# Down projection of a hybrid decoder layer: GpSimd forms the sums of weights, the products of doubly summed weights stand last, the last trip has one seven-product block, and the start has fewer constant matmuls

## The chip, the cores and the metric

The kernel runs on one core of one Trainium2 chip. The time is device microseconds (us) of one execution. Engines are named as in the profile: PE is TensorE (matmuls; PEld its weight loads), DVE is VectorE, ACT is ScalarE, POOL is GpSimd, SP is the engine that issues the DMAs.

## The reference

One pre-norm decoder layer over 256 tokens, all in float32: three token mixers on one input projection, gates, an output projection with residual, then a squared-ReLU MLP with residual and a final RMS norm. The change lies in the last line but one, in its second product.

```python
h = rmsnorm(x, norm_ffn_g[l])
x = x + jnp.square(jax.nn.relu(h @ w_up[l])) @ w_down[l]     # 256x2048 @ 2048x8192, 256x8192 @ 8192x2048
return rmsnorm(x, final_g)
```

## The kernel before

**Weights.** All weights stream through a ring of four slots of 128x1024 float32 (512 KB, a "slab"). SP loads slab s into `w_raw[s % 4]` (line 412 or 415) once DVE has finished the low part of slab s - 4 (semaphore `lo_done`). ACT rounds the slab to the fast matmul type, `w_hi` (line 503; line 501 for half a slab), DVE takes the rest, `w_lo = w_raw - w_hi` (line 729; line 726 for half), and PE multiplies high by high, high by low and low by high: three matmuls for each product. ACT and DVE prepare slab k + 3 in the step in which PE multiplies slab k. ACT may overwrite a slot of `w_hi` when PE reports the slab used (`slab_used`).

**The MLP.** The 8192 hidden columns are done in 4 chunks of 2048. A chunk has 4 trips of `up` (8 slabs each) and 2 trips of `down` (16 slabs each), so there are 8 down trips in all. A down trip makes 1024 output columns in two column groups n = 0 and 1, and takes its 16 slabs (n, i) in the order of `PAIR` and `PAIR_ENDS`.

**Blocks of seven products.** At steps k = 6, 10 and 14 of a down trip (`quads`; in the last trip 6 and 10 only) the slabs k and k + 1 hold the same rows of both column groups. With the two row tiles of each and the two token tiles they make a 2 by 2 by 2 block product, which is done with seven products (P1 to P7) in place of eight, in Strassen's manner: 21 matmuls of 128x512 in place of 24. `products_quad` issues them. Four of the products need sums of weights, `w_sums`, called T1, T3, T2, T4: T1 and T3 are differences of loaded weights (one 128x1024 operation, `forms_first`), T2 is made from T1 and T4 from T2 (a 128x512 operation each, `forms_second`). ACT rounds them two at a time (`forms_hi`, lines 509 and 511), DVE takes the rest (`forms_lo`, line 756, semaphore `t_lo`, two counts for each block). P5 uses T1, P7 uses T3, P6 uses T2, P4 uses T4.

**Order of the work.** Everything is written by hand, engine by engine, and runs in program order on each engine. In the block that closes a trip (k = 14), P2, P4 and P3 come first, since they finish the four accumulators of the ordinary products (`c_full`), which DVE empties (`corner_sums`, line 790) before the next trip writes them; the other four products end in banks that `token_sums` (lines 772 to 783) empties after the block.

**The start.** Six constant matmuls stand before the first two groups of transposes of x and `WARM_GAP` = 20 of them (line 1400) between the second and the third group.

Of the kernel before, what the change touches and what calls it, by code (L numbers as in the profile page):

```python
# [141 lines left out]
def pair_of(c, t):  # L142

    return c * PH["down"].trips + t
# [15 lines left out]
WARM_GAP = 20  # L160
# [48 lines left out]
def build(nc, x, norm_mix_g, w_in, gate_b, conf_dw, conf_ln_g, conf_ln_b, w_conf_out, sconv_w,  # L209
# [5 lines left out]
    with ctx:  # L215
# [132 lines left out]
        def wide_rows(slab):  # L348

            return slab.rearrange("p (k b) n -> p k (b n)", k=DKT)  # L350
# [26 lines left out]
        def _(sp):  # L377
# [4 lines left out]
            def load_slab(ph, c, t, k):  # L382
# [102 lines left out]


        @block.scalar
        def _(act):
# [228 lines left out]
        def _(dve):  # L717
# [13 lines left out]
            def forms_first(ph, c, t, k):  # L731

                x, y = k % RING, (k + 1) % RING
                quad = quad_of(ph, c, t, k)
                if not (isinstance(quad, int) and quad == 0):
                    dve.wait_ge(t_lo, quad * 2)
                dve.wait_ge(raw_full[x], raw_count(ph, c, t, k))
                dve.wait_ge(raw_full[y], raw_count(ph, c, t, k + 1))
                left = w_raw[:, x:x + 2, 0:2, :].rearrange("p s k b -> p s (k b)")
                dve.tensor_tensor(w_sums[:, T1:T3 + 1, :], wide_rows(w_raw[:, y]), left, ALU.subtract).then_inc(t_raw, 1)  # L740

            def forms_second(ph, c, t, k):

                x, y = k % RING, (k + 1) % RING
                quad = quad_of(ph, c, t, k)
                dve.wait_ge(t_raw, quad * 2 + 1)
                dve.tensor_tensor(w_sums[:, T2, :], half_rows(w_raw[:, y], 1), w_sums[:, T1, :],
                                  ALU.subtract).then_inc(t_two, 1)
                dve.wait_ge(t_two, quad + 1)
                dve.tensor_tensor(w_sums[:, T4, :], half_rows(w_raw[:, x], 1), w_sums[:, T2, :],  # L750
                                  ALU.subtract).then_inc(t_raw, 1)

            def forms_lo(ph, c, t, k, part):
                dve.wait_ge(t_hi, quad_of(ph, c, t, k) * 2 + part + 1)
                two = slice(2, 4) if part == 0 else slice(0, 2)
                dve.tensor_tensor(w_forms[:, 1, two, :], w_sums[:, two, :], w_forms[:, 0, two, :].bitcast(F32),
                                  ALU.subtract).then_inc(t_lo, 1)
# [291 lines left out]
            def trip(ph, c, t):  # L1049
# [4 lines left out]
                for k in range(ph.nslabs):  # L1054
# [15 lines left out]
                    if k + 3 in quads(ph, c, t):  # L1070
                        forms_second(ph, c, t, k + 3)
# [3 lines left out]
                    if k + 4 in quads(ph, c, t):  # L1075
                        forms_first(ph, c, t, k + 4)
# [190 lines left out]
        def _(pe):  # L1267
# [58 lines left out]
            def products_quad(ph, c, t, k):  # L1326
# [22 lines left out]

                pe.wait_ge(lo_done, s + 1)  # L1350
                product(4, whole(0, 2 * i + 1), loaded(w_x, 1), False, closing)
                pe.wait_ge(t_lo, quad * 2 + 1)
                last = product(5, whole(1, 2 * i + 1), summed(T4), False, closing)
                if closing:
                    last.then_inc(c_full, 1)
                pe.wait_ge(lo_done, s + 2)
                pe.wait_ge(f_lo, c * 4 + i // 2 + 1)
                last = product(6, form(S4), loaded(w_y, 1), False, closing)
                if closing:
                    last.then_inc(c_full, 1)  # L1360
                if first and not (isinstance(c, int) and c == 0 and isinstance(t, int) and t == 0):
                    pe.wait_ge(p_sum, pair_of(c, t) * P_SUMS)
                product(P_BANK["P1"], whole(0, 2 * i), loaded(w_x, 0), first, final).then_inc(slab_used, 1)
                product(P_BANK["P6"], form(S2), summed(T2), first, final)
                pe.wait_ge(t_lo, quad * 2 + 2)
                product(P_BANK["P7"], form(S3), summed(T3), first, final)
                product(P_BANK["P5"], form(S1), summed(T1), first, final).then_inc(slab_used, 1)
# [208 lines left out]
```

## Time and profile before

| | |
|---|---|
| median of 3 runs | 1520.77 us (1520.45 to 1520.98) |
| the profiled execution's own time | 1521.96 us |
| its span, first to last instruction | 1519.9 us |
| PE busy | 1505.6 us |
| PEld busy | 1270.0 us |
| DVE busy | 1190.9 us |
| ACT busy | 756.1 us |
| POOL busy | 2.0 us |
| mean granted TensorE clock | 0.998 |

A row of the timeline gives the start and the duration in us from the span's start, the engine, the line of the kernel, what is written and read, and in brackets how long the engine had been idle and which event ended that. A PE row lasts longer than its share of the engine, since matmuls are pipelined: the distance between starts is what one costs.

### The profile page before, as it was taken

To read this page: it belongs to the slowest core of one execution; us is meant where nothing else is said; L and a number is where in the kernel's file an instruction comes from. 1 tells how busy PE (TensorE), PEld (TensorE's weight loads), DVE (VectorE), ACT (ScalarE), POOL (GpSimd) and SP (SyncE) were. 2 spreads that over 40 slices of the span, in tenths; PEclk is the share of its full clock that TensorE was granted. 3 is DMA by queue.
4 is the path that set the end of the run, shared out by engine and by line. 5 is a ranking of instruction groups with operands and counts; after the bars stand their busy time and mean duration, and the time that the engine had idled before them with its cause. 6 is when DMAs were issued, how large, how long until landed. Compare 5 with 4: busy or idle time off the path is not lost. (4 is left out here: it accounts for less than half of the span.)

```text
span 1519.9 us, 22403 instructions
## 1 busy us (share of the span) xinstructions
PE 1505.6 (99%) x7670; PEld 1270.0 (84%) x7670; DVE 1190.9 (78%) x1578; ACT 756.1 (50%) x942; POOL 2.0 (0%) x11
## 2 busy tenths in 40 slices
PE   9999999999999999999999999999999999999997
PEld 8888888877778888888888888888888888888885
DVE  6568888988889877565556779987798779887798
ACT  5544444465554455444445445545455545544553
POOL 0000000000000000000000000000000000000000
PEclk9999999999999999999999999999999999999999
DMA  7655566655556556656555655655656565566553
GB/s 240 194 180 190 187 195 199 196 182 173 171 171 193 194 194 211 194 195 199 181 180 171 197 186 208 207 190 170 207 190 211 170 211 199 181 196 203 204 198 138
DMA packets 209961, 290.86 MB, mean 191 GB/s; under 512 B 9227, under 2 KB 129107, under 8 KB 209778
## 3 DMA queue, kind: packets, MB, share of 16 engines
q1 hardware_dynamic: 209906, 290.14, 58.2%
q8 instruction: 33, 0.54, 0.2%
q14 instruction: 22, 0.18, 0.0%
HBM read 287.48 MB, written 2.10 MB: 191 GB/s over the span
## 5 line engine op out<-in xcount | busy, mean ns | idle before, releaser
L503 ACT ACTIVATE w_hi<-w_raw 128x1024 fp32r<-128x1024 f32 x510 | 532.8, 1056 | 458.0 <-PE acc L1321 266.2
L729 DVE TENSOR_TENSOR w_lo<-w_raw,w_hi 128x1024 fp32r<-128x1024 f32 x510 | 614.6, 1221 | 170.6 <-ACT w_hi L503 165.8
L1297 PE MATMUL acc<-h_hl,w_hi 128*128 128x512 f32 x1740 | 546.7, 395 | 0.0
L1295 PEld LDWEIGHTS acc<-h_hl,w_lo 128*128 128x128 f32 x1740 | 322.3, 188 | 72.7 <-issue 0.6
L1295 PE MATMUL acc<-h_hl,w_lo 128*128 128x256 f32 x1740 | 343.6, 279 | 0.0
L1297 PEld LDWEIGHTS acc<-h_hl,w_hi 128*128 128x128 f32 x1740 | 265.2, 189 | 0.0
L1319 PE MATMUL acc<-w_hi,m_hl 128*128 128x512 f32 x456 | 177.8, 390 | 0.0
L1321 PE MATMUL acc<-w_hi,m_hl 128*128 128x512 f32 x456 | 177.4, 389 | 0.0
L1320 PE MATMUL acc<-w_lo,m_hl 128*128 128x512 f32 x456 | 177.4, 389 | 0.0
L1319 PE MATMUL acc<-w_hi,h_hl 128*128 128x512 f32 x384 | 151.5, 394 | 0.0
L1321 PE MATMUL acc<-w_hi,h_hl 128*128 128x512 f32 x384 | 149.6, 389 | 0.0
L1320 PE MATMUL acc<-w_lo,h_hl 128*128 128x512 f32 x384 | 149.5, 389 | 0.0
L869 DVE SCALAR_TENSOR_TENSOR conv<-glu,par,conv (+1 forms) x240 | 108.8, 479 | 7.0 <-DVE conv L869 5.8
L1321 PEld LDWEIGHTS acc<-w_hi,m_hl 128*128 128x128 f32 x456 | 85.6, 188 | 17.8
L1320 PEld LDWEIGHTS acc<-w_lo,m_hl 128*128 128x128 f32 x456 | 85.6, 188 | 17.7
L1319 PEld LDWEIGHTS acc<-w_hi,m_hl 128*128 128x128 f32 x456 | 85.6, 188 | 17.6
L1319 PEld LDWEIGHTS acc<-w_hi,h_hl 128*128 128x128 f32 x384 | 72.1, 188 | 17.1 <-DVE w_lo L729 2.7
L661 ACT ACTIVATE second<-acc 128x512 f32<-128x512 f32 x58 | 34.7, 599 | 102.6 <-PE acc L1297 102.6
L1321 PEld LDWEIGHTS acc<-w_hi,h_hl 128*128 128x128 f32 x384 | 72.1, 188 | 15.2
L1320 PEld LDWEIGHTS acc<-w_lo,h_hl 128*128 128x128 f32 x384 | 72.1, 188 | 14.4
L1191 DVE TENSOR_TENSOR pair<-acc,second 128x512 f32<-128x512 f32 x54 | 37.3, 691 | 55.0 <-ACT second L661 54.9
L698 ACT ACTIVATE m_hl<-pair 128x512 f32 (+1 forms) x32 | 20.2, 632 | 74.1 <-DVE pair L1242 74.1
(202 smaller groups left out, 1472.8 us busy)
## 6 DMA issues: line engine op xcount, KB each, us to landing
w_raw<-in_w_in SPq DMA_DIRECT2D x200, 512.0 KB, 3.5
w_raw<-in_w_up SPq DMA_DIRECT2D x128, 512.0 KB, 4.3
w_raw<-in_w_down SPq DMA_DIRECT2D x128, 512.0 KB, 4.4
w_raw<-in_w_mix_out SPq DMA_DIRECT2D x32, 512.0 KB, 3.6
w_raw<-in_w_sconv_out SPq DMA_DIRECT2D x16, 512.0 KB, 4.2
w_raw<-in_w_attn_out SPq DMA_DIRECT2D x16, 512.0 KB, 3.9
w_raw<-in_w_conf_out SPq DMA_DIRECT2D x16, 512.0 KB, 4.2
bias_row<-in_gate_b SPq DMA_DIRECT2D x12, 256.0 KB, 3.9
```

Source lines behind the costliest of these rows:

```text
L503: act.activation(w_hi[:, q], w_raw[:, q], ACT.Copy).then_inc(hi_done, 1)
L661: act.activation(second[:, :, :], acc[:, b:b + 2, SEQ:], ACT.Copy).then_inc(half_copied, 1)
L698: act.activation(m_hl[:, bass.ds(j * 2, 2), 0, :], pair[n][:, :, :], ACT.Copy).then_inc(hid_hi, 1)
L729: dve.tensor_tensor(w_lo[:, q], w_raw[:, q], w_hi[:, q].bitcast(F32), ALU.subtract).then_inc(lo_done, 1)
L869: dve.scalar_tensor_tensor(dst, src, w, dst, ALU.mult, ALU.add).then_inc(step, 1)
L1191: dve.tensor_tensor(dst, halves[0], second[:, :, :], ALU.add).then_inc(half_sum, 1)
L1295: pe.matmul(*narrow[m], start=False, stop=False)
L1297: last = pe.matmul(*wide[m], start=False, stop=final)
L1319: pe.matmul(acc[:, b + m, :], h_h, hi[:, a, :], start=first, stop=False)
L1320: pe.matmul(acc[:, b + m, :], h_h, lo[:, a, :], start=False, stop=False)
L1321: last = pe.matmul(acc[:, b + m, :], h_l, hi[:, a, :], start=False, stop=final)
```

## The change

The two operations of `forms_first` and `forms_second` move from DVE to POOL, which runs them for every block in a stream of its own, as soon as both slabs have landed and `forms_lo` has consumed the sums before. DVE keeps a wait for them: before it takes the low part of slab k + 3 in step k = block - 2. The loads of slab block + 4 (and of the third slab of each up or down trip) wait for one more `lo_done`, since POOL may still read the slot. ACT and DVE now round T1 and T3 first, T2 and T4 second. `products_quad` has a new order: in the blocks at k = 6 and 10 it is P2, P1, P3, P7, P5, P6, P4; in the closing block P2, P4, P3, P1, P7, P5, P6. The last trip has one block (k = 10) and treats slabs 6 and 7 with ordinary products. `WARM_GAP` is 6.

```diff
-    return (6, 10) if last_trip(ph, c, t) else (6, 10, 14)
+    return (10,) if last_trip(ph, c, t) else (6, 10, 14)
...
-WARM_GAP = 20
+WARM_GAP = 6
...
+                late = k - RING in quads(ph, c, t) or ph.name in ("up", "down") and k == 2
                 if not (isinstance(s, int) and s < RING or shared and k == KDOWN):
-                    sp.wait_ge(lo_done, s + (shared and k == KDOWN - 1) - (RING - 1))
+                    sp.wait_ge(lo_done, s + (shared and k == KDOWN - 1) + late - (RING - 1))
...
@@ block.gpsimd
+            def forms_first(ph, c, t, k):
+                x, y = k % RING, (k + 1) % RING
+                quad = quad_of(ph, c, t, k)
+                if not (isinstance(quad, int) and quad == 0):
+                    pool.wait_ge(t_lo, quad * 2)
+                pool.wait_ge(raw_full[x], raw_count(ph, c, t, k))
+                pool.wait_ge(raw_full[y], raw_count(ph, c, t, k + 1))
+                left = w_raw[:, x:x + 2, 0:2, :].rearrange("p s k b -> p s (k b)")
+                pool.tensor_tensor(w_sums[:, T1:T3 + 1, :], wide_rows(w_raw[:, y]), left, ALU.subtract).then_inc(t_raw, 1)
+
+            def forms_second(ph, c, t, k):
...
+                pool.wait_ge(t_raw, quad * 2 + 1)
+                pool.tensor_tensor(w_sums[:, T2, :], half_rows(w_raw[:, y], 1), w_sums[:, T1, :],
+                                  ALU.subtract).then_inc(t_two, 1)
+                pool.wait_ge(t_two, quad + 1)
+                pool.tensor_tensor(w_sums[:, T4, :], half_rows(w_raw[:, x], 1), w_sums[:, T2, :],
+                                  ALU.subtract).then_inc(t_raw, 1)
...
@@ forms_hi, ACT
                 if k + 2 in quads(ph, c, t):
-                    act.wait_ge(t_raw, quad_of(ph, c, t, k + 2) * 2 + 2)
+                    act.wait_ge(t_raw, quad_of(ph, c, t, k + 2) * 2 + 1)
+                    act.activation(w_forms[:, 0, 0:2, :], w_sums[:, 0:2, :], ACT.Copy).then_inc(t_hi, 1)
+                if k + 1 in quads(ph, c, t):
+                    act.wait_ge(t_raw, quad_of(ph, c, t, k + 1) * 2 + 2)
                     act.activation(w_forms[:, 0, 2:4, :], w_sums[:, 2:4, :], ACT.Copy).then_inc(t_hi, 1)
-                if k + 1 in quads(ph, c, t):
-                    act.activation(w_forms[:, 0, 0:2, :], w_sums[:, 0:2, :], ACT.Copy).then_inc(t_hi, 1)
...
@@ trip, DVE
-                    if k + 3 in quads(ph, c, t):
-                        forms_second(ph, c, t, k + 3)
+                    if k + 2 in quads(ph, c, t):
+                        dve.wait_ge(t_raw, quad_of(ph, c, t, k + 2) * 2 + 2)
                     if ph.name == "down" and k == 15 and not last_trip(ph, c, t):
                         corner_sums(c, t)
                     lo(ph, c, t, k)
-                    if k + 4 in quads(ph, c, t):
-                        forms_first(ph, c, t, k + 4)
...
@@ products_quad, PE
+                pe.wait_ge(lo_done, s + 1)
+                corner("P2")
+                if closing:
+                    corner("P4").then_inc(c_full, 1)
+                    corner("P3").then_inc(c_full, 1)
+                    shared("P1").then_inc(slab_used, 1)
+                    shared("P7")
+                    shared("P5")
+                    shared("P6").then_inc(slab_used, 1)
+                else:
+                    shared("P1").then_inc(slab_used, 1)
+                    corner("P3")
+                    shared("P7")
+                    shared("P5")
+                    shared("P6")
+                    corner("P4").then_inc(slab_used, 1)
```

In the new `products_quad`, P4 and P6 wait for `t_lo` at the block's second count, P7 and P5 at its first. Before, P4 waited for the first count and P7 for the second.

DVE's order in the first down trip, before the change, from the preparation of slab 6 to the second `forms_lo` of the block at k = 6 and on to the sums of the next block:

```order
L740 TENSOR_TENSOR w_sums<-w_raw 128x1024 [waits raw_full3,raw_full2]
L747 TENSOR_TENSOR w_sums<-w_raw,w_sums 128x512 [waits t_raw]
L750 TENSOR_TENSOR w_sums<-w_raw,w_sums 128x512 [waits t_two]
L729 TENSOR_TENSOR w_lo<-w_raw,w_hi 128x1024 [waits hi_done]
L726 TENSOR_TENSOR w_lo<-w_raw,w_hi 128x512 [waits hi_done]
L756 TENSOR_TENSOR w_forms<-w_sums,w_forms 128x1024 [waits t_hi]
L729 TENSOR_TENSOR w_lo<-w_raw,w_hi 128x1024 [waits hi_done]
L756 TENSOR_TENSOR w_forms<-w_sums,w_forms 128x1024 [waits t_hi]
L729 TENSOR_TENSOR w_lo<-w_raw,w_hi 128x1024 [waits hi_done]
L740 TENSOR_TENSOR w_sums<-w_raw 128x1024 [waits raw_full3,raw_full2,t_lo]
```

The same stretch of DVE after the change (`t_raw` is POOL's report that the sums are there):

```order
L766 TENSOR_TENSOR w_lo<-w_raw,w_hi 128x512 [waits hi_done,t_raw]
L774 TENSOR_TENSOR w_forms<-w_sums,w_forms 128x1024 [waits t_hi]
L769 TENSOR_TENSOR w_lo<-w_raw,w_hi 128x1024 [waits hi_done]
L774 TENSOR_TENSOR w_forms<-w_sums,w_forms 128x1024 [waits t_hi]
L769 TENSOR_TENSOR w_lo<-w_raw,w_hi 128x1024 [waits hi_done] x2
L766 TENSOR_TENSOR w_lo<-w_raw,w_hi 128x512 [waits hi_done,t_raw]
```

The three operations on `w_sums` have left DVE; the half slab's low part, on which the load of slab block + 5 waits, now waits for POOL's last sum, and both `forms_lo` stand behind it.

PE's first seven matmuls of the closing block of the first down trip, before:

```order
L1346 MATMUL acc<-w_hi,m_hl 128x512 [waits lo_done,hid_lo]
L1347 MATMUL acc<-w_lo,m_hl 128x512
L1348 MATMUL acc<-w_hi,m_hl 128x512
L1346 MATMUL acc<-w_forms,m_hl 128x512 [waits t_lo]
L1347 MATMUL acc<-w_forms,m_hl 128x512
L1348 MATMUL acc<-w_forms,m_hl 128x512
L1346 MATMUL acc<-w_hi,a_forms 128x512 [waits f_lo,lo_done]
```

and after:

```order
L1362 MATMUL acc<-w_hi,m_hl 128x512 [waits lo_done,hid_lo]
L1363 MATMUL acc<-w_lo,m_hl 128x512
L1364 MATMUL acc<-w_hi,m_hl 128x512
L1362 MATMUL acc<-w_forms,m_hl 128x512 [waits t_lo]
L1363 MATMUL acc<-w_forms,m_hl 128x512
L1364 MATMUL acc<-w_forms,m_hl 128x512
L1362 MATMUL acc<-w_hi,a_forms 128x512 [waits f_lo,lo_done]
```

P4 (the rows with `w_forms,m_hl`) stays the second product of the closing block. What has changed is the count of `t_lo` for which it waits: the first `forms_lo` before, the second now.

## Rows read from the trace of the kernel before

**Rows 1.** The page's busy times (engine, us, share, instructions)

```profile
PE 1505.6 (99%) x7670; PEld 1270.0 (84%) x7670; DVE 1190.9 (78%) x1578; ACT 756.1 (50%) x942; POOL 2.0 (0%) x11
```

**Rows 2.** Waits of PE's weight loads: total us, times, longest

```profile
PEld acc L1346 <- DVE w_forms L756: 3.7, 4, 2.1
```

**Rows 3.** DVE's timeline in the first down trip

```profile
917.18 1.23 DVE L740 TENSOR_TENSOR w_sums<-w_raw 128x1024 f32<-128x1024 f32 x1 [1.81 <-DMA w_raw<-in_w_down]
...
919.16 0.69 DVE L750 TENSOR_TENSOR w_sums<-w_raw,w_sums 128x512 f32<-128x512 f32 x1
...
920.90 0.68 DVE L726 TENSOR_TENSOR w_lo<-w_raw,w_hi 128x512 fp32r<-128x512 f32 x1
921.51 1.22 DVE L756 TENSOR_TENSOR w_forms<-w_sums,w_forms 128x1024 fp32r<-128x1024 f32 x1
922.64 1.22 DVE L729 TENSOR_TENSOR w_lo<-w_raw,w_hi 128x1024 fp32r<-128x1024 f32 x1
...
926.53 1.22 DVE L740 TENSOR_TENSOR w_sums<-w_raw 128x1024 f32<-128x1024 f32 x1 [0.40 <-DMA w_raw<-in_w_down]
...
930.26 0.69 DVE L726 TENSOR_TENSOR w_lo<-w_raw,w_hi 128x512 fp32r<-128x512 f32 x1
...
936.04 1.23 DVE L740 TENSOR_TENSOR w_sums<-w_raw 128x1024 f32<-128x1024 f32 x1 [0.55 <-DMA w_raw<-in_w_down]
...
940.37 1.22 DVE L756 TENSOR_TENSOR w_forms<-w_sums,w_forms 128x1024 fp32r<-128x1024 f32 x1
...
942.64 1.22 DVE L756 TENSOR_TENSOR w_forms<-w_sums,w_forms 128x1024 fp32r<-128x1024 f32 x1
...
948.64 0.68 DVE L772 TENSOR_TENSOR y_tok<-p_part,y_tok 128x512 f32<-128x512 f32 x1
```

**Rows 4.** PE's timeline in the same trip, around its three blocks

```profile
922.35 0.39 PE L1346 MATMUL acc<-w_hi,m_hl 128*128 128x512 f32 x1
...
932.55 0.39 PE L1346 MATMUL acc<-w_hi,m_hl 128*128 128x512 f32 x1
...
942.75 0.39 PE L1346 MATMUL acc<-w_hi,m_hl 128*128 128x512 f32 x1
...
943.43 0.39 PE L1346 MATMUL acc<-w_forms,m_hl 128*128 128x512 f32 x1
...
947.51 0.39 PE L1319 MATMUL acc<-w_hi,m_hl 128*128 128x512 f32 x1
```

**Rows 5.** DMA issues of line 412: ns min/median/max

```profile
L412 SPq DMA_DIRECT2D w_raw<-in_w_down x128: 367/372/382, 891.9 to 1492.9; - x128
```

**Rows 6.** A later trip: DVE's sums for its closing block, and PE there

```profile
1324.46 1.23 DVE L740 TENSOR_TENSOR w_sums<-w_raw 128x1024 f32<-128x1024 f32 x1 [0.87 <-DMA w_raw<-in_w_down]
...
1329.99 0.39 PE L1346 MATMUL acc<-w_hi,m_hl 128*128 128x512 f32 x1
```

**Rows 7.** POOL's groups: xcount | busy us, mean ns

```profile
L477 POOL MEMSET mask<- 128x384 f32 x1 | 0.4, 418 | 0.0
...
L475 POOL TENSOR_SCALAR_AFFINE_SELECT ident<-ident 128x128 f32<-128x128 f32 x1 | 0.3, 292 | 0.1
...
L1566 POOL MEMSET const-float32-1.0<- 128x1 f32 x1 | 0.1, 98 | 0.0
```

**Rows 8.** PE's timeline, first block of the last trip

```profile
1487.44 0.50 PE L1346 MATMUL acc<-w_forms,a_forms 128*128 128x512 f32 x1 [1.65 <-DVE w_forms L756]
```

**Rows 9.** Timelines of PE and DVE at the start

```profile
7.04 4.66 PE L1400 MATMUL acc<-ident,ones 128*128 128x128 f32 x40
11.53 1.04 PE L1370 MATMUL acc<-ident,y_tok 128*128 128x128 f32 x8
12.32 0.70 PE L1290 MATMUL acc<-h_hl,w_hi 128*128 128x512 f32 x2
...
9.09 1.23 DVE L822 TENSOR_TENSOR w_lo<-w_raw,w_hi 128x1024 fp32r<-128x1024 f32 x1
```

**Rows 10.** Loads of x: from issue to landing, five DMAs, issued 1.2 to 4.9

```profile
DMA to landing us min/median/max: 2.7/6.3/9.7
```

**Rows 11.** Busy by stretch: us, PE, PEld, DVE, ACT, POOL, PEclk

```profile
1510.00:1512.00 2.00, 0.18 (x1) 0.00 (x0) 1.83 (x7) 1.09 (x4) 0.00 (x0) 1.00 0.01 4
```

More of the change, by code:

```diff
@@ L484, in _, with trip @@
                                fill=MASKED, base=-1, pattern=[[1, BLK]], channel_multiplier=-1).then_inc(consts, 1)
+            def forms_first(ph, c, t, k):
[8 more added lines that the diff above has]
+            def forms_second(ph, c, t, k):
+                x, y = k % RING, (k + 1) % RING
+                quad = quad_of(ph, c, t, k)
+                pool.wait_ge(t_raw, quad * 2 + 1)
[4 more added lines that the diff above has]
+                                  ALU.subtract).then_inc(t_raw, 1)
+            def trip(ph, c, t):
+                if ph == "v tokens":
+                    return
+                for k in quads(ph, c, t):
+                    forms_first(ph, c, t, k)
+                    forms_second(ph, c, t, k)
+            trip(PH["down"], 0, 0)
+            with pool.Fori(1, PH["down"].trips) as t:
+                trip(PH["down"], 0, t)
+            with pool.Fori(1, CHUNKS - 1) as c:
+                with pool.Fori(0, PH["down"].trips) as t:
+                    trip(PH["down"], c, t)
+            for t in range(PH["down"].trips):
+                trip(PH["down"], CHUNKS - 1, t)
         @block.scalar
@@ L729, in lo @@
                     dve.tensor_tensor(w_lo[:, q], w_raw[:, q], w_hi[:, q].bitcast(F32), ALU.subtract).then_inc(lo_done, 1)
[L731 to L751, printed above, removed]
             def forms_lo(ph, c, t, k, part):
                 dve.wait_ge(t_hi, quad_of(ph, c, t, k) * 2 + part + 1)
-                two = slice(2, 4) if part == 0 else slice(0, 2)
+                two = slice(0, 2) if part == 0 else slice(2, 4)
                 dve.tensor_tensor(w_forms[:, 1, two, :], w_sums[:, two, :], w_forms[:, 0, two, :].bitcast(F32),
@@ L1348, in product, with corner @@
                     return pe.matmul(acc[:, at, :], rows[1], columns[0], start=False, stop=stop)
+                def corner(name):
+                    if name == "P2":
+                        return product(4, whole(0, 2 * i + 1), loaded(w_x, 1), False, closing)
+                    if name == "P3":
+                        pe.wait_ge(lo_done, s + 2)
+                        pe.wait_ge(f_lo, c * 4 + i // 2 + 1)
+                        return product(6, form(S4), loaded(w_y, 1), False, closing)
+                    pe.wait_ge(t_lo, quad * 2 + 2)
+                    return product(5, whole(1, 2 * i + 1), summed(T4), False, closing)
@@ new lines, in shared @@
+                def shared(name):
+                    if name == "P1":
+                        if first and not (isinstance(c, int) and c == 0 and isinstance(t, int) and t == 0):
+                            pe.wait_ge(p_sum, pair_of(c, t) * P_SUMS)
+                        return product(P_BANK[name], whole(0, 2 * i), loaded(w_x, 0), first, final)
+                    rows, f = {"P6": (S2, T2), "P7": (S3, T3), "P5": (S1, T1)}[name]
+                    pe.wait_ge(t_lo, quad * 2 + (2 if name == "P6" else 1))
+                    return product(P_BANK[name], form(rows), summed(f), first, final)
@@ L1350, in products_quad @@
                 pe.wait_ge(lo_done, s + 1)
-                product(4, whole(0, 2 * i + 1), loaded(w_x, 1), False, closing)
-                pe.wait_ge(t_lo, quad * 2 + 1)
-                last = product(5, whole(1, 2 * i + 1), summed(T4), False, closing)
+                corner("P2")
                 if closing:
[L1355 to L1366, printed above, removed]
```

1 line of the change is left out of this document (removed).

## The prediction

> **What bounds the kernel now.** I read the page first: PE is busy 1505.6 us of a span of 1519.9 [rows 1], and the rest lies at the two ends, so PE is the bound and the time changes where PE issues fewer matmuls or waits. The view of waits comes second. In all 23 blocks together PE's weight loads wait 3.7 us for `w_forms` [rows 2]; the largest stall of the matmuls, 1.65 us, is in the first block of the last trip [rows 8]. So there is little to win; what decides is whether the new order keeps PE fed.
>
> The DVE timeline of the first down trip beside PE's [rows 3, 4] shows how near the edge this is. The blocks start at 922.35, 932.55 and 942.75: 10.20 us apart, for 21 and 24 matmuls, so a matmul costs 10.20 / 45 = 0.227 us and a product of three 0.68. DVE's sums for them start at 917.18, 926.53 and 936.04, each time just as the second slab of the block lands (the DMA ends the idle time). These landings hang in a loop: slab 11 is loaded when the low part of slab 7 is done (920.90 + 0.68 = 921.58) and lands at 926.53, 4.95 later; slab 15 hangs on slab 11 in the same way (930.95 to 936.04, 5.09). The loop takes 9.35 to 9.5 us a turn, PE 10.20 a block: it has 0.7 to 0.85 us in hand per turn. At the closing block P4 starts at 943.43 and the `forms_lo` it needs ended at 940.37 + 1.22 = 941.59, 1.84 us earlier.
>
> **The sums on POOL.** The trace has no two-input operation of POOL, so the cost X of the three operations is bounded from both sides. As fast as DVE: 1.23 + 0.69 + 0.69, which the rows put from 917.18 to 919.85, 2.7 us. POOL's own rows [rows 7] are 98 ns for a memset of one element a partition, 418 for 384 (0.84 ns an element written) and 292 for an affine_select of 128, one input and one output: (292 - 98) / 128 = 1.52 ns an element. By that rate the 1024, 512 and 512 elements take 3 x 0.1 + 2048 x 0.00152 = 3.4 us. A second input is one more stream; at the price of the memset's stream, 0.84, the rate is 2.36 and X = 0.3 + 4.8 = 5.1 us. I take 5.1, since the operations do have two inputs and the nearest row has one; both ends stay for the range.
>
> The Trainium skill's page "GPSIMD Engine Reference", section 3.1, gives 4497 ns for a two-input operation of 2048 float32. Scaled to these sizes, an estimate from that page is X = 4.7, and the sum below would come to about 1547 in place of 1555.
>
> **What becomes of the loop.** In step block - 2 DVE now waits for POOL's last sum, then does the half slab, `forms_lo`, a slab, `forms_lo`. By the distances in [rows 3] (0.61, 1.13, 1.14 and 1.22 for the last) the half slab ends 0.68 and the second `forms_lo` 4.10 us after the sums. Both loads of the next block now wait for that half slab, so slab 11 is issued behind slab 10: 0.37 us more [rows 5], 5.3 us to landing. In the times of the first trip, with X = 5.1:
>
> - Block at 6: slab 7 lands 917.18 as before (it hangs on slab 3, untouched). Sums 922.28, half slab 922.96, second `forms_lo` 926.38. P6 is the sixth product and would start at 922.35 + 3.40 = 925.75: PE is 0.63 late.
> - Block at 10: landing 928.26, sums 933.36, half slab 934.04, second `forms_lo` 937.46, against 932.55 + 3.40 = 935.95: 1.5 late in all.
> - Closing block: landing 939.34, sums 944.44, second `forms_lo` 948.54. P4 is second here and needs it; it would start at 943.43: 5.1 us late in all.
>
> The turn is 5.3 + 5.1 + 0.7 = 11.1 us, slower than PE's 10.20, and P4 waits for the later of the two `forms_lo` where it waited for the earlier. The last block's end moves with 3X. In other trips the third landing is later against PE: 1329.99 - 1324.46 = 5.5 us ahead of the closing block [rows 6] against 6.7 in the first. Between them I add 0.4: 5.5 us a trip, 38.5 us in the 7 trips with three blocks. Three of these trips follow another down trip; there the late `token_sums` has been the brake on slab 3. They start 948.64 - 947.51 = 1.1 us after PE's end now; DVE has then also more time to be ready, about 0.5 us after PE's end, so 3 x 0.6 = 1.8 us comes back. Down trips cost +36.7 us.
>
> What DVE saves (2.7 us a block) buys nothing: it stands at the wait for POOL in that time. ACT's two roundings of sums keep their places; the first is ready before DVE needs it, the second before the second `forms_lo`, since a slab's low part stands between. The extra wait of the third slab's load in up and down trips is hidden: ACT wants that slab three steps of 2.72 us later, and a landing takes some 5.
>
> **The last trip.** Three more matmuls, +0.68; the wait of its first block goes, 1.65 idle plus 0.11 on the slower matmul, -1.8. Its one block at k = 10 is not behind a loop (slab 7 needs no sums), so POOL has time: slab 11 lands 5.3 us after the low part of slab 7, some 8 us ahead of the block. Together -1.1 us.
>
> **The start.** 40 rows of constant matmuls take 4.66 us, 28 of them 3.3 [rows 9]. The third part of x is issued at 2.7 and lands 6.3 later, at 9.0 [rows 10]; the transposes, now at 11.53, can start there and need 0.8. The first product then waits for the first low part, 9.09 + 1.23 = 10.32, and starts at about 10.4 in place of 12.32: -1.9 us, which the later slabs keep, since ACT and DVE move up with the transposes. It costs more than it gains only if the idle moments (8.4 to 9.0, 9.9 to 10.4) drop the clock. At the end of the program PE's last matmul ended at 1510.2 and the granted clock was still 1.0 up to 1512 [rows 11], so pauses of 0.6 us are short beside what it bore there.
>
> **Sum.** 36.7 - 1.1 - 1.9 = +33.7 on the profiled 1521.96, 1555.7; the median of the runs lies 1.2 below the profiled execution, so 1554.5, rounded to 1555.
>
> **Rivals.**
> - *POOL and DVE hold each other up.* Just before the second slab of a block lands, the first has landed and DVE takes its low part (1.22 us); if the two cannot run together, POOL starts some 1.0 us late in the second and third block, 2 us a trip, 14 us in all: 1569 with X = 5.1. For it: the two meet in every trip. Against it: no row of before has both busy. The Trainium skill's page "SBUF — State Buffer", "Who interferes with whom", says that a DVE instruction with two SBUF inputs and a GpSimd instruction that reads SBUF exclude each other, the later one waiting in full; that is this mechanism, and no row of before can show it. With the page's X as well the estimate would be about 1561.
> - *POOL is quick enough* (the other side). From X = 3.4 down the first trip's P4 is on time: 948.54 - 3 x 1.7 = 943.44 against 943.43. Then what is left is a second `forms_lo` that follows the low part of slab 16; in before it ended at 942.64 + 1.22 = 943.86 [rows 3], 0.4 after P4's start, and it can hardly be earlier than 943.5. So 7 x 0.1 to 0.4 is lost, 3.0 won at the ends and up to 0.9 from the waits of before: 1517.5 to 1520.5. For it: no row shows a slow POOL. Against it: already its one-input rate gives 3.4.
> - *The waits fall elsewhere*, so that the same X costs half: if slabs 10 and 11 land faster than 5 us, the loop has 0.5 us more a turn, 1 us a trip: 1548. It is in the range of the forecast.
>
> **Numbers.** POOL at 4.2 to 5.5 without mutual blocking, 1537 to 1563: 0.52. With blocking, 1556 to 1574: 0.33. POOL quick: 0.13, half of it within 0.2% (3 us, about what a measurement can tell from no change), half faster. Something else: 0.02. The range 1537 to 1572 leaves out the quick POOL and a little at the top. Faster 0.08, same 0.07, slower 0.85.
>
> **What would show it.** POOL's three operations take near 5 us for a block, not 2.7. PE waits for `w_forms` at the fourth matmul of the closing block in seven trips, 3 to 6 us of delay summed over each trip, and DVE's half slab waits for POOL. Slab 11 lands about 5.3 us after the half slab of 7. In the last trip no wait; the first product starts near 10.4 at full clock. If DVE rows of 128x1024 last over 1.3 us, or POOL's first sum starts later than its slab lands, the two block each other. I am wrong if X is below 3.5, or if POOL's sums start much earlier than the landings that DVE waits for now.

## The result, and the profile after

The changed kernel takes 1592.44 us (median of 4 runs, 1589.84 to 1594.64) against 1520.88 (1520.45 to 1522.96) before, on the same chip: a ratio of 1.0461, 95% interval 1.0449 to 1.0474. It is slower, as forecast, but by 71.6 us where 34 were forecast, and outside the range. The profiled executions differ by 68.1 us of span (1588.0 against 1519.9).

The page gives the busy times [rows 1 before] and the 40 slices of the span. A slice is 39.7 us, and the down trips lie from about 912 us on.

```profile
PE 1527.1 (96%) x7645; PEld 1273.9 (80%) x7645; DVE 1134.5 (71%) x1507; ACT 754.6 (48%) x940; POOL 120.2 (8%) x77
...
PE   9999999999999999999999989899889998899987
...
POOL 0000000000000000000000043001230012400121
```

PE's slices are below 9 only in the down part, eight of them, and in seven of the eight POOL has work. PE is "busy" for 21 us more with 25 matmuls fewer: some of them ran slower. The view of waits (engine, line, what is waited for: total us, times, longest) answers [rows 2]:

```profile
DVE w_lo L766 <- POOL w_sums L506: 115.8, 22, 6.0
...
PEld acc L1362 <- DVE w_forms L774: 55.4, 32, 5.3
...
PE acc L1362 <- DVE w_forms L774: 41.3, 23, 4.9
...
PE acc L1362 <- DVE w_lo L766: 5.7, 9, 1.3
```

DVE's half slab stands 22 times for POOL's last sum, and PE's weight loads stand 55.4 us for `w_forms`, 3.7 before. The 5.7 us for `w_lo` L766 is P3, waiting for the half slab, a wait that the prediction did not have. POOL's timeline in the first down trip shows the loop:

```profile
915.48 2.44 POOL L496 TENSOR_TENSOR w_sums<-w_raw 128x1024 f32<-128x1024 f32 x1 [912.71 <-DMA w_raw<-in_w_down]
917.99 1.30 POOL L503 TENSOR_TENSOR w_sums<-w_raw,w_sums 128x512 f32<-128x512 f32 x1
919.37 1.30 POOL L506 TENSOR_TENSOR w_sums<-w_raw,w_sums 128x512 f32<-128x512 f32 x1
926.97 3.18 POOL L496 TENSOR_TENSOR w_sums<-w_raw 128x1024 f32<-128x1024 f32 x1 [6.30 <-DMA w_raw<-in_w_down]
...
939.35 3.15 POOL L496 TENSOR_TENSOR w_sums<-w_raw 128x1024 f32<-128x1024 f32 x1 [6.42 <-DMA w_raw<-in_w_down]
```

and DVE's beside it, which answers to [rows 3]:

```profile
920.71 0.69 DVE L766 TENSOR_TENSOR w_lo<-w_raw,w_hi 128x512 fp32r<-128x512 f32 x1 [5.68 <-POOL w_sums L506]
...
926.63 1.22 DVE L769 TENSOR_TENSOR w_lo<-w_raw,w_hi 128x1024 fp32r<-128x1024 f32 x1 [0.69 <-ACT w_hi L542]
...
932.96 0.69 DVE L766 TENSOR_TENSOR w_lo<-w_raw,w_hi 128x512 fp32r<-128x512 f32 x1 [5.10 <-POOL w_sums L506]
...
938.98 1.22 DVE L769 TENSOR_TENSOR w_lo<-w_raw,w_hi 128x1024 fp32r<-128x1024 f32 x1 [0.79 <-ACT w_hi L542]
...
945.29 0.69 DVE L766 TENSOR_TENSOR w_lo<-w_raw,w_hi 128x512 fp32r<-128x512 f32 x1 [5.08 <-POOL w_sums L506]
...
948.17 1.22 DVE L774 TENSOR_TENSOR w_forms<-w_sums,w_forms 128x1024 fp32r<-128x1024 f32 x1
```

The three sums take 919.37 + 1.30 - 915.48 = 5.19 us. The half slab ends at 920.71 + 0.69 = 921.40, and the next sums start when the slab lands, 926.97: 5.57 later (5.70 in the next turn, 933.65 to 939.35). The turns are 11.49 and 12.38 us, against PE's 10.20. In the second and third block POOL's first sum starts while DVE is in the 1.22 us low part that began 0.34 and 0.37 us earlier, and lasts 3.18 and 3.15 in place of 2.44. Over the 14 turns of the seven trips with three blocks the turn is 12.29 us in the mean (11.49 to 13.08; 9.68 before), and the leg from the half slab's end to the landing is 6.12 (5.57 to 6.99; before, with the load issued alone, 5.27). The first trip is one of the milder ones. PE's timeline beside it, which answers to [rows 4]:

```profile
924.86 0.51 PE L1362 MATMUL acc<-w_forms,a_forms 128*128 128x512 f32 x1 [0.62 <-DVE w_forms L774]
...
933.70 0.50 PE L1362 MATMUL acc<-w_hi,a_forms 128*128 128x512 f32 x1 [0.38 <-DVE w_lo L766]
...
934.84 0.50 PE L1362 MATMUL acc<-w_forms,a_forms 128*128 128x512 f32 x1 [0.17 <-DVE w_forms L774]
...
937.11 0.50 PE L1362 MATMUL acc<-w_forms,a_forms 128*128 128x512 f32 x1 [0.61 <-DVE w_forms L774]
...
944.49 0.39 PE L1364 MATMUL acc<-w_hi,m_hl 128*128 128x512 f32 x1
949.44 0.79 PE L1362 MATMUL acc<-w_forms,m_hl 128*128 128x512 f32 x1 [4.56 <-DVE w_forms L774]
950.03 0.63 PE L1363 MATMUL acc<-w_forms,m_hl 128*128 128x512 f32 x1
950.46 0.63 PE L1364 MATMUL acc<-w_forms,m_hl 128*128 128x512 f32 x1
```

P6 is late in block 6, P3, P7 and P6 in block 10, and P4 in the closing block starts 949.44 - 944.49 - 0.23 = 4.72 us late; the five delays (start to start, less 0.227 for a matmul) add to 7.2 us. Behind P4 the matmuls stand 0.43 us apart in place of 0.227. The windows show why (the stretch, its length, busy of PE, PEld, DVE, ACT, POOL, then the granted clock; 1.00 is 2.4 GHz, 0.50 is 1.2 GHz; the last two are the share and GB/s of the DMAs):

```profile
941.00:944.00 3.00, 3.00 (x15) 2.49 (x14) 0.00 (x0) 1.47 (x2) 2.84 (x3) 1.00 0.13 51
944.00:949.00 5.00, 0.88 (x4) 0.38 (x3) 3.71 (x4) 2.54 (x3) 1.25 (x1) 1.00 0.33 97
949.00:952.40 3.40, 2.96 (x7) 2.38 (x8) 2.75 (x3) 0.00 (x0) 0.00 (x0) 0.50 0.95 357
952.40:956.00 3.60, 3.60 (x17) 2.96 (x17) 2.89 (x3) 2.26 (x3) 0.00 (x0) 1.00 0.29 111
```

PE was idle for 4.56 us, and the clock was at its lower level from 949.0 to 952.4. That happens at P4's wait in each of the seven trips with a closing block, beginning between 2.9 us before P4's start and 0.7 behind it, for 3.4 us in four of them and 6.8 us in three. By the distances between the starts of PE's matmuls in the down part, delays of over 0.06 us add to 60.4 us (3.1 before), and the slower matmuls to 11.0 us (0 before). This count takes in the matmul behind each late one, which is late too, by 0.11 us, or by 0.36 at the lower clock; with these the first trip has 8.0 us, not 7.2.

At the start the prediction's step held: twelve constant matmuls end early, the transposes start at 9.47 (9.0 was given), and the first product at 10.49 (12.32 in [rows 9]).

```profile
7.02 1.50 PE L1433 MATMUL acc<-ident,ones 128*128 128x128 f32 x12
9.47 1.09 PE L1403 MATMUL acc<-ident,y_tok 128*128 128x128 f32 x8 [0.95 <-DMA y_tok<-in_x]
10.49 0.70 PE L1306 MATMUL acc<-h_hl,w_hi 128*128 128x512 f32 x2
```

### The profile page after: what moved, and what is told of

Its sections match the earlier page's. It is cut to its first block and busy times, and to the rows that moved or that the text cites. A ratio compares the mean times of both kernels' runs of the same rounds, so it can differ in the third digit from the quotient of the medians.

```text
span 1588.0 us, 22392 instructions
## 1 busy us (share of the span) xinstructions
PE 1527.1 (96%) x7645; PEld 1273.9 (80%) x7645; DVE 1134.5 (71%) x1507; ACT 754.6 (48%) x940; POOL 120.2 (8%) x77
## 5 line engine op out<-in xcount | busy, mean ns | idle before, releaser
L1335 PE MATMUL acc<-w_hi,m_hl 128*128 128x512 f32 x464 | 180.9, 390 | 0.0
L1336 PE MATMUL acc<-w_lo,m_hl 128*128 128x512 f32 x464 | 180.6, 389 | 0.0
L1337 PE MATMUL acc<-w_hi,m_hl 128*128 128x512 f32 x464 | 180.6, 389 | 0.0
L496 POOL TENSOR_TENSOR w_sums<-w_raw 128x1024 f32<-128x1024 f32 x22 | 60.0, 2727 | 1436.2 <-DMA w_raw<-in_w_down 1436.2
L766 DVE TENSOR_TENSOR w_lo<-w_raw,w_hi 128x512 fp32r<-128x512 f32 x22 | 15.2, 693 | 115.8 <-POOL w_sums L506 115.8
(202 smaller groups left out, 1519.9 us busy)
```

Of the source, the lines that this page charges most:

```text
L496: pool.tensor_tensor(w_sums[:, T1:T3 + 1, :], wide_rows(w_raw[:, y]), left, ALU.subtract).then_inc(t_raw, 1)
L766: dve.tensor_tensor(half_rows(w_lo[:, q], 1), half_rows(w_raw[:, q], 1), half_rows(w_hi[:, q], 1).bitcast(F32), ALU.subtract).then_inc(lo_ ...
L1335: pe.matmul(acc[:, b + m, :], h_h, hi[:, a, :], start=first, stop=False)
L1336: pe.matmul(acc[:, b + m, :], h_h, lo[:, a, :], start=False, stop=False)
L1337: last = pe.matmul(acc[:, b + m, :], h_l, hi[:, a, :], start=False, stop=final)
```

## The experiments

Each time is a median, with its ratio to the kernel before, run beside it on the same chip (1522.99 to 1523.39 us). The changed kernel was run beside a before of 1520.88, so differences between it and the others are taken from the ratios (0.1% is 1.5 us). "Stalls" are the delays between matmul starts in the down part, counted as for the 60.4 us above, and "clock" is what the slower matmuls add, 11.0 there; both are of the one profiled execution.

### Which part of the change costs

**e1_ends_only**: the kernel before with the two changes at the ends.

```diff
-    return (6, 10) if last_trip(ph, c, t) else (6, 10, 14)
+    return (10,) if last_trip(ph, c, t) else (6, 10, 14)
-WARM_GAP = 20
+WARM_GAP = 6
```

> The kernel before with two parts of the change alone: 6 constant matmuls in place of 20 at the start, and one block in place of two in the last trip. My step: -1.9 us at the start and -1.1 us in the last trip, so about 1517.9 us (-0.2%). Rival: the pauses of PE at the start drop the clock, and the start gains nothing or loses up to 3 us, 1520 to 1523.

1519.76 us, 0.9976 (0.9967 to 0.9986): a gain of some 3.7 us; the prediction had 3.0.

**e2_sums_on_dve**: the changed kernel with `forms_first` and `forms_second` back on DVE, in their old places.

```diff
-                    if k + 2 in quads(ph, c, t):
-                        dve.wait_ge(t_raw, quad_of(ph, c, t, k + 2) * 2 + 2)
+                    if k + 3 in quads(ph, c, t):
+                        forms_second(ph, c, t, k + 3)
...
+                    if k + 4 in quads(ph, c, t):
+                        forms_first(ph, c, t, k + 4)
```

> The changed kernel with the three operations on sums of weights back on DVE in their old places; order of roundings, order of products, later loads and both ends as in the changed kernel. If POOL's slowness is the cause: only P4 of the closing block waits, for a second forms_lo that ended 0.4 to 1.7 us after P4's start in the trace of before, 0.9 a trip, 6.4 us in all, less 3 at the ends: 1522 to 1526 us. Rival, the new orders and the later loads are the cause: 1570 us or more.

1541.46 us, 1.0121 (1.0106 to 1.0137). So POOL is the larger part of the loss, 1.0461 against 1.0121 or 52 us, but 18 us are lost without it, which neither theory had. DVE's timeline of the same trip:

```profile
915.36 1.23 DVE L742 TENSOR_TENSOR w_sums<-w_raw 128x1024 f32<-128x1024 f32 x1 [1.74 <-DMA w_raw<-in_w_down]
...
925.36 1.23 DVE L742 TENSOR_TENSOR w_sums<-w_raw 128x1024 f32<-128x1024 f32 x1 [1.05 <-DMA w_raw<-in_w_down]
...
935.48 1.23 DVE L742 TENSOR_TENSOR w_sums<-w_raw 128x1024 f32<-128x1024 f32 x1 [1.17 <-DMA w_raw<-in_w_down]
...
942.08 1.22 DVE L758 TENSOR_TENSOR w_forms<-w_sums,w_forms 128x1024 fp32r<-128x1024 f32 x1
```

The turns are 10.00 and 10.12 us, where [rows 3] has 9.35 and 9.51. And P4 waits for the `forms_lo` that ends at 943.30:

```profile
941.17 0.39 PE L1350 MATMUL acc<-w_hi,m_hl 128*128 128x512 f32 x1
943.36 0.50 PE L1348 MATMUL acc<-w_forms,m_hl 128*128 128x512 f32 x1 [1.80 <-DVE w_forms L758]
...
944.96 0.63 PE L1348 MATMUL acc<-w_hi,m_hl 128*128 128x512 f32 x1
945.38 0.63 PE L1349 MATMUL acc<-w_lo,m_hl 128*128 128x512 f32 x1
```

A wait of 1.80 us was enough to be followed by matmuls 0.42 us apart. In this kernel the clock fell in four of the seven trips, behind delays of P4 of 1.95 to 2.7 us (start to start); behind the other three, 1.7 to 2.5 us, it did not. Stalls 18.2, clock 5.6.

**e9_later_loads_only**: the kernel before with the later loads. **e10_new_orders_on_dve**: e2 without them.

```diff
+                late = k - RING in quads(ph, c, t) or ph.name in ("up", "down") and k == 2
-                    sp.wait_ge(lo_done, s + (shared and k == KDOWN - 1) - (RING - 1))
+                    sp.wait_ge(lo_done, s + (shared and k == KDOWN - 1) + late - (RING - 1))
```

> The kernel before with the later loads alone (slab block + 4, and the third slab of each up or down trip, wait for one more lo_done). In e2 each turn of the loop from load to load was 0.65 us longer than before, 1.3 us by the closing block. In the kernel before P4 has 0.6 to 1.8 us in hand there, so this alone costs 0 to 2 us in all: 0 to +0.1%. Rival, the later loads cost by themselves what e2 lost: +8 us or more.

> e2 without the later loads: sums on DVE, new orders of roundings and products, both ends. P4 of the closing block waits for the second forms_lo, 0.4 to 1.7 us late, 6.4 us in all, and the ends give 3.6: +2 to +4 us against before (+0.1 to +0.3%), with the clock at 1.0 as no stall reaches 2 us. e2 lies at +1.2%; the difference of some 15 us is then what the later loads cost once P4 has no slack. Rival, the new order alone costs it: e10 at +1% or more.

e9: 1533.93 us, 1.0071 (1.0057 to 1.0085), where next to nothing was expected. e10: 1525.85 us, 1.0021 (1.0012 to 1.0030), as expected. With e2 they close the account of its 18 us. Against e1 the new orders cost 0.45%, 7 us, most of it P4's wait for the second `forms_lo` (stalls 6.6 against 1.8), and on top of that the later loads cost 1.0%, 15 us. In e9 they alone cost 11. The clock is enough to explain the difference: it costs 5.6 us in e2 and nothing in e9. Its turns, again by DVE's timeline:

```profile
917.41 1.23 DVE L741 TENSOR_TENSOR w_sums<-w_raw 128x1024 f32<-128x1024 f32 x1 [1.78 <-DMA w_raw<-in_w_down]
...
927.37 1.23 DVE L741 TENSOR_TENSOR w_sums<-w_raw 128x1024 f32<-128x1024 f32 x1 [1.00 <-DMA w_raw<-in_w_down]
...
937.28 1.23 DVE L741 TENSOR_TENSOR w_sums<-w_raw 128x1024 f32<-128x1024 f32 x1 [0.95 <-DMA w_raw<-in_w_down]
```

They are 9.96 and 9.91 us, 0.4 to 0.6 longer than before. Over the seven trips the landing leg is 5.92 us in the mean, 5.27 before, and eight of the 14 turns take longer than PE's 10.20 (11.09 at most).

**e13_late_in_down_only** and **e14_late_third_slab_only** split the later loads:

```diff
+                late = k - RING in quads(ph, c, t)               # e13
+                late = ph.name in ("up", "down") and k == 2      # e14
```

> Half of e9 on the kernel before: only the loads of slab block + 4 wait for one more lo_done. If e9's loss (+0.7%) comes from the longer turn of the load loop, it is all here: +0.5 to +0.8%. Rival, it comes from the third slab of each trip, which is loaded when DVE is busy with the end of the trip before: 0 to +0.2% here.

> The other half: only the third slab of each up and down trip waits for one more lo_done. By the longer turn of the load loop: 0 to +0.2%. By the rival (the third slab): +0.5 to +0.8%.

e13: 1532.83 us, 1.0062 (1.0049 to 1.0076), stalls 10.8. e14: 1524.25 us, 1.0005 (0.9996 to 1.0014). All of the loss is in the loads of slab block + 4; the wait of the third slab is hidden, as predicted.

### How much of it is POOL's duration

**e3_three_quarters** and **e4_half**: the changed kernel, in which POOL forms the sums for 384 or 256 of the 512 columns of each. The other columns of the sums are left out (they hold zeros).

```diff
-                pool.tensor_tensor(w_sums[:, T1:T3 + 1, :], wide_rows(w_raw[:, y]), left, ALU.subtract).then_inc(t_raw, 1)
+                pool.tensor_tensor(w_sums[:, T1:T3 + 1, 0:256], wide_rows(w_raw[:, y])[:, :, 0:256], left[:, :, 0:256], ALU.subtract).then_inc(t_raw, 1)
```

> The changed kernel with POOL working on 384 of each 512 columns (the sums of the other columns are left out and stand at zero). Everything else as changed. By the lengths of POOL's operations in the changed kernel (2.44 and 1.30 us, so 2.2 ns an element and 0.16 a call) the three take 4.1 us in place of 5.2. With the loop as the cause each trip is 3 x 1.1 = 3.4 us less late, about 4 us, no single stall is near 4.5 us and the clock stays at 1.0: 7 x 4 - 5 = +24 us, 1540 to 1550. Rival, a fixed cost of handing the sums between engines: 1570 us or more.

> The same with 256 of each 512 columns: POOL's three operations take 2.9 us, about what DVE needed. The loop then turns faster than PE, and the time falls to 1518 to 1524 us, near the kernel before. Rival, a fixed cost of handing over: the step from 384 to 256 columns brings as little as that from 512 to 384 did not, over 1550 us.

e3: 1570.83 us, 1.0319 (1.0303 to 1.0334). e4: 1537.25 us, 1.0090 (1.0074 to 1.0105). Both are well above what was expected, since the expectations had neither the cost of the later loads nor the clock. The time follows POOL's duration: three operations take 5.2 us, 4.1 (e3) and 2.95 (e4) where DVE is not beside them, and the ratios are 1.0461, 1.0319 and 1.0090. The steps are 22 and 35 us for a quarter each. POOL's timeline of e4:

```profile
917.94 1.31 POOL L496 TENSOR_TENSOR w_sums<-w_raw 128x512 f32<-128x512 f32 x1 [915.17 <-DMA w_raw<-in_w_down]
919.33 0.75 POOL L503 TENSOR_TENSOR w_sums<-w_raw,w_sums 128x256 f32<-128x256 f32 x1
...
927.35 2.05 POOL L496 TENSOR_TENSOR w_sums<-w_raw 128x512 f32<-128x512 f32 x1 [6.45 <-DMA w_raw<-in_w_down]
```

The second of the two large sums is again 0.7 us longer, though it has half the elements: what is added comes from DVE's operation and is no share of POOL's.

### POOL and DVE beside each other

**e12_no_dve_beside_pool**: the changed kernel, in which DVE takes the low part of slabs 10 and 14, the ones before the sums of the second and third block, for a single element of each partition; the rest of these low parts is left out.

```diff
+                elif k + LOOKAHEAD in (10, 14) and k + LOOKAHEAD in quads(ph, c, t):
+                    dve.tensor_tensor(w_lo[:, q, 0, 0:1], w_raw[:, q, 0, 0:1], w_hi[:, q, 0, 0:1].bitcast(F32),
+                                      ALU.subtract).then_inc(lo_done, 1)
```

> The changed kernel in which DVE's operation that meets POOL's first one (the low part of slabs 10 and 14 of a down trip) is cut to one element a partition; that part of the low weights is left out. If the two block each other and that has a price, POOL's first operation takes 2.45 us in all blocks and the half slab comes 0.7 us earlier in each turn, 1.4 us a trip, 10 us in 7 trips, some more if the clock falls for shorter: 1574 to 1584 us. Rival, the blocking hides behind other waits: 1590 us or more.

1583.11 us, 1.0389 (1.0373 to 1.0405), 0.7% or 11 us below the changed kernel, with an uncertainty of some 3 us. POOL's group of line 496 (xcount | busy us, mean ns), in e12:

```profile
L496 POOL TENSOR_TENSOR w_sums<-w_raw 128x1024 f32<-128x1024 f32 x22 | 54.4, 2472 | 1435.2 <-DMA w_raw<-in_w_down 1435.2
```

and in the changed kernel:

```profile
L496 POOL TENSOR_TENSOR w_sums<-w_raw 128x1024 f32<-128x1024 f32 x22 | 60.0, 2727 | 1436.2 <-DMA w_raw<-in_w_down 1436.2
```

POOL's operations are 5.6 us shorter in all, the profiled executions differ by 6.2 us of span (1588.0 and 1581.8), and the medians by 11. The rest need not be blocking: the mean clock was 0.983 to 0.987 in the runs of the changed kernel, with the profiled run at the upper end, and 0.987 to 0.989 in those of e12. The turns of the first trip are 11.6 and 11.7 without the second party (11.49 and 12.38 with it).

In the last trip of the changed kernel the two hold each other up in turn, first POOL behind DVE, then DVE behind POOL, then POOL again:

```profile
1553.86 3.08 POOL L496 TENSOR_TENSOR w_sums<-w_raw 128x1024 f32<-128x1024 f32 x1 [28.57 <-DMA w_raw<-in_w_down]
1555.61 2.41 DVE L769 TENSOR_TENSOR w_lo<-w_raw,w_hi 128x1024 fp32r<-128x1024 f32 x1 [0.97 <-ACT w_hi L542]
1557.02 2.17 POOL L503 TENSOR_TENSOR w_sums<-w_raw,w_sums 128x512 f32<-128x512 f32 x1
```

Without a meeting these take 2.44, 1.22 and 1.30 us. It is the sign that the prediction named, a DVE row of over 1.3 us.

**e6_dve_waits_earlier**: DVE waits for the sums one step earlier, so it has nothing to do while POOL works.

```diff
-                    if k + 2 in quads(ph, c, t):
-                        dve.wait_ge(t_raw, quad_of(ph, c, t, k + 2) * 2 + 2)
+                    if k + 3 in quads(ph, c, t):
+                        dve.wait_ge(t_raw, quad_of(ph, c, t, k + 3) * 2 + 2)
```

> The changed kernel; DVE waits for POOL's sums one slab earlier, so that no DVE operation runs beside POOL's first operation in the second and third block. If the two block each other on SBUF, POOL's operation of 128x1024 takes 2.45 us in all blocks, where it took 3.15 in the second and third; DVE's slab now stands behind it (1.14 us more to the half slab), so the time is a little worse than 1592, up to 1600. Rival, POOL's longer operation comes from the DMA landing beside it or from the data: it stays at 3.1 us in the second and third block.

1608.60 us, 1.0556 (1.0538 to 1.0573). POOL's first sum is at its short duration throughout, as expected:

```profile
929.34 2.44 POOL L496 TENSOR_TENSOR w_sums<-w_raw 128x1024 f32<-128x1024 f32 x1 [7.63 <-DMA w_raw<-in_w_down]
...
943.51 2.45 POOL L496 TENSOR_TENSOR w_sums<-w_raw 128x1024 f32<-128x1024 f32 x1 [8.95 <-DMA w_raw<-in_w_down]
```

But the turns are 12.84 and 14.17 (12.8 to 14.2 in all trips): the low part that had run beside POOL now runs behind it, and more loads hang on it. So it is no remedy, and the time was missed.

### The orders and the clock

**e5_old_order_pool**: the changed kernel with the old order of ACT's and DVE's roundings of the sums and of PE's products (P4 waits for the first `forms_lo` again; POOL's part and the loads stay).

```diff
-                corner("P2")
+                product(4, whole(0, 2 * i + 1), loaded(w_x, 1), False, closing)
+                pe.wait_ge(t_lo, quad * 2 + 1)
+                last = product(5, whole(1, 2 * i + 1), summed(T4), False, closing)
```

> The changed kernel with the old order of roundings (T2 and T4 first) and the old order of products in every block; POOL still makes the sums, ends and later loads as changed. P4 of the closing block then waits for the first forms_lo, which ends about 2.3 us after the sums, not 4.1. With the loop as the cause each trip is 1.8 us less late and no stall is as long as 4.5 us, so the clock falls less: 12 us from the order and up to 14 from the clock, 1565 to 1580 us. Rival, the order of products is worth nothing since POOL is late anyway: 1590 us.

1577.18 us, 1.0348 (1.0331 to 1.0366): 17 us better than with the new orders (stalls 46.9, clock 9.9), as expected.

**e8_p4_later_in_closing**: P4 after P5 in the closing block.

```diff
                 if closing:
-                    corner("P4").then_inc(c_full, 1)
-                    corner("P3").then_inc(c_full, 1)
                     shared("P1").then_inc(slab_used, 1)
+                    corner("P3")
                     shared("P7")
                     shared("P5")
+                    corner("P4").then_inc(c_full, 2)
```

> The changed kernel with P4 sixth in place of second in the closing block (P2, P1, P3, P7, P5, P4, P6); both corner banks are reported with it. P4 then starts 2.7 us later on PE's side, so each trip is 2.7 us less late at P4 and the longest stall is near 2 us, so the clock holds; in exchange DVE empties the first two banks (1.2 us) about 1 us after the block ends and PE waits for that. 7 x (2.7 + 2 of clock - 1.5) = 22 us less: 1565 to 1577 us. Rival, the wait only moves to the emptying of the banks: 1585 us or more.

1573.45 us, 1.0324 (1.0307 to 1.0342), with a mean clock of 0.998. The stalls are 51.1 us, 9 less than in the changed kernel, but in pieces of 1.5 us at most, and the clock doesn't fall in the down trips. Together that is 21 us by the ratios.

**e7_zero_matmuls**: 16 matmuls with zero weights ahead of P4 in the closing block, added work that changes no sum.

```diff
+                    pe.wait_ge(zero_ok, 1)
+                    for _ in range(16):
+                        pe.matmul(acc[:, 5, :], zeros[:, :], half_rows(w_hi[:, w_x], 1), start=False, stop=False)
```

> The changed kernel with 16 matmuls of zero weights (added to the accumulator that P4 uses, so they add zero) in PE's stall of the closing block, 3.6 us of PE work in a stall of 4.6 to 5.1. If the stall drops the clock and that is part of the loss, the granted clock is 1.0 throughout and the time falls by 1.5 to 3 us a trip, to 1573 to 1582 us. Rival, the clock's fall costs nothing beside the stall: 1592 us, clock 0.985 or 1.0.

1579.51 us, 1.0370 (1.0352 to 1.0387), mean clock 0.998. The PE timeline of the closing block:

```profile
945.21 3.89 PE L1392 MATMUL acc<-w_hi,zeros 128*128 128x512 f32 x16
949.95 0.50 PE L1364 MATMUL acc<-w_forms,m_hl 128*128 128x512 f32 x1 [0.86 <-DVE w_forms L775]
```

The waiting is the same: P4 starts at 949.95 (949.44 in the changed kernel), and the remaining delays with the 112 zero matmuls, 34.9 + 25.4 us, come to 60.3. Yet 14 us are won by the ratios, 10.6 us by the spans of the profiled executions: that is the price of the clock, and the distances between matmuls (11.0) say the same.

**e11_ends_and_p4_fourth**: e1 with P4 fourth, after P3, in the blocks that don't close a trip.

```diff
+                else:
+                    shared("P1").then_inc(slab_used, 1)
+                    corner("P3")
+                    corner("P4")
+                shared("P6")
```

> The kernel before with both ends of the change, and with P1 and P3 ahead of P4 in the blocks that don't close a trip (P2, P1, P3, P4, P6, P7, P5; old roundings, sums on DVE). It takes away the waits of P4 in the first block of some trips, 0.2 to 0.65 us in four trips: 1.4 us less than e1, so -0.3% against before. Rival, those waits reappear at the closing block: the same as e1, -0.24%.

1519.27 us, 0.9978 (0.9968 to 0.9987): not to be told from e1. These two are the versions that beat both kernels, by the ends alone.

## Why the prediction was wrong in size

**The ends: right.** "Together -1.1 us" and "-1.9 us" were the terms; e1 measured -3.7 us for both. The start's mark is at 10.49 where 10.4 was given.

**The sums on POOL: right.** X was taken as 5.1; alone the three take 5.2. The two parts of the 5.1 were each a little off: 2.44 us for 1024 elements and 1.30 for 512 are 2.2 ns an element, not 2.36, and 0.16 us each time, not 0.1, with 0.08 between two operations. The estimate from the Trainium skill's page "GPSIMD Engine Reference", section 3.1, was 4.7. The trace agrees with that page's 4497 ns for 2048 elements, 2.2 ns each; what the estimate lacked is the fixed part of three operations.

**The mechanism and the place: right.** The loop of release, load and sums is what is slower than PE, P4 of the closing block is where most of it is paid, and the third slab's load is hidden. In the first block P6 is late by 0.79 (0.63 given).

**The step that failed is the size of the loop's turn**, "5.3 + 5.1 + 0.7 = 11.1 us", and with it "5.5 us a trip". The turn measured 12.29 us in the mean of 14, and the stalls 60.4 / 7 = 8.6 us a trip. Two terms carry most of it:
- *The landing leg, 5.3.* It took 6.12 us in the mean. The first trip, from which the term was read, has short ones, 5.57 and 5.70. In the kernel before they were 4.95 and 5.09 there, but 5.27 in the mean of 14 and 6.07 at most; the turns were 9.25 to 10.48, 9.68 in the mean. So the kernel before had 0.5 us "in hand" a turn, not 0.7 to 0.85, and once less than nothing. The later loads alone lengthen the leg to 5.92 (e9), by 0.65 us where 0.37 was given. Why it is 0.65 stays open: both loads then run together, which the runs don't separate from the issue. The last step, from 5.92 to 6.12, stays open too.
- *Mutual blocking.* It was left out of the sum and given to a rival, at +1.0 for the second and third block, 14 us. It is there, and it is smaller. In the 14 such blocks POOL's first sum met a DVE operation eleven times: it was 0.7 to 0.85 us longer in six, 0.2 to 0.5 in three, 0.1 in two, and 2.44 us in the three without a meeting. That is 5.7 us in all; with what else comes back, e12 gives 6 (profiled executions) to 11 us (medians). The Trainium skill's page "SBUF — State Buffer", section "Who interferes with whom", says that such a pair excludes each other and the later one waits in full. The trace agrees nearly: 926.63 + 1.22 = 927.85 is 0.88 after POOL's start, and POOL's operation is 0.74 longer. With the last trip and a first block that makes 13 meetings in all, and in each the first sum is longer by what was left of DVE's operation, less 0.13 to 0.15 us. The "against it" in the prediction, that no row showed both busy, was an absence of evidence, and with a rule on hand that speaks against the change its chance should have been above one half.

**A step that was missing: the clock.** The prediction weighed pauses of 0.6 us at the start and forecast a stall of 3 to 6 us at P4 without asking what the clock does behind it. It costs 14 us by e7, 11 by the distances. [Rows 11] were read as saying that an idle PE keeps its clock up to 1512; they say so for 2 us behind the last matmul at 1510.2, and nothing for 4.7. The next stretch of the same trace of before had the answer, a granted clock of 0.68 and then 0.50, with PE idle:

```profile
1512.00:1513.00 1.00, 0.00 (x0) 0.00 (x0) 0.96 (x4) 0.59 (x3) 0.00 (x0) 0.68 0.02 8
1513.00:1519.90 6.90, 0.00 (x0) 0.00 (x0) 1.92 (x4) 1.32 (x2) 0.00 (x0) 0.50 0.76 304
```

**A wait that was missing, at no price: P3.** In the block at k = 10 P3 needs the half slab of slab 11, which is now behind POOL. P3 is 0.54 us late in the first trip and up to 1.45 in the others, and P7 and P6 are late again behind it; the prediction counted at P4 and P6 alone. But this is the same lateness met earlier. All 22 times POOL's first sum waits for the load and the half slab for POOL's last sum (the rows above), never for PE, so by this reading what PE loses at P3 it no longer loses at P4. The surcharge for the later trips, 0.4 us over the first, was nearly right: 8.6 against 8.0 on the same count.

**The account.** By the profiled executions, from 33.7 us forecast to 68.1: over the 14 turns the landing leg adds 14 x 0.82 = 11.5 us, the blocking 5.7, the 0.1 us more of X in 21 blocks 2, and the half slab, which ends 0.73 us behind the sums in three trips and 0.88 in four where 0.7 was given, 2.4. That is 21.7 on the 38.5 us forecast for the seven trips, 60.2, where the stalls are 60.4 (3.1 before). The clock adds 11. Some 2 us are left over, about the 1.8 us that the forecast took off at the start of three trips: the stalls come out without them. The durations are read from the trace of the changed kernel; that the load's later issue, the blocking and the clock are causes is shown by e9 and e13, by e12 and e6, and by e7. The medians lie 3.5 us further apart than the profiled executions (71.6), and there the mean clock is lower. P4's wait for the second `forms_lo` was in the forecast; the old order is worth 17 us in e5. Effects add only where PE already waits: the later loads cost 11 us alone and 15 beside the new orders, where the longer stalls also drop the clock.

## What to carry to other kernels

When a resource is released later, write down the whole turn of the loop (release, issue, landing, use) and compare it with the consumer's turn in several trips, not only in the first: here 0.5 us of slack a turn, in the mean of all trips, was all that stood between "hidden" and 10 us. An operation handed to an idle engine is paid in that engine's duration on the path, 5.2 us against 2.7 here, plus what it and its neighbour take from each other. A forecast stall on PE of some microseconds needs a second term for the clock behind it; spread the wait over several products, or fill it, before trying to shorten it.

## What the runs showed of the hardware

- A two-input subtraction on POOL took 2.44 us for 1024 float32 a partition, 1.30 for 512 and 0.75 for 256, against 1.23 and 0.69 on DVE. When it started inside a two-input subtraction of DVE it became longer by what was left of that one less 0.13 to 0.15 us, up to 0.85 in all (13 meetings), and by the same rule at 512 elements (e4, 2.05 us in place of 1.31). A DVE subtraction that started inside one of POOL took 2.41 us in place of 1.22.
- P4's delays of 4.6 to 5.1 us came with the lower clock level (0.50) in all seven trips, for 3.4 or 6.8 us; delays of 1.7 to 2.7 us came with it in four of seven trips (e2). With delays of at most 1.5 us, spread over the block, it did not fall (e8), nor with zero-weight matmuls in the wait (e7). Behind the last matmul of the kernel before, which ended at 1510.2, it was 1.00 up to 1512 and 0.50 from 1513.
- At that level a matmul of 512 columns cost 0.42 to 0.43 us in place of 0.227.
- From the release of its buffer to its landing a 512 KB load took 5.27 us in the mean when it was issued alone (before), and 5.92 when the load before it was held back and issued with it (e9).
